# A fp32 decoder trunk on one core: x in five transfers among the first weights, raw rows paired and new queries placed by ScalarE, the norm of x at its old tiles

## The reference

```python
def project_layer(x, pos, norm_g, w_in):
    h = rms_norm(x, norm_g) @ w_in
    pr = dict(zip(IN_NAMES, jnp.split(h, IN_OFFSETS, axis=-1)))
    q_a = rope(pr['q_a'].reshape(b, t, N_DIL * A_HEADS, HEAD_DIM), pos)
    k_a = rope(pr['k_a'].reshape(b, t, N_DIL * A_KV, HEAD_DIM), pos)
    q_c = rope(pr['q_c'].reshape(b, t, C_HEADS, HEAD_DIM), pos)
    kv_c = pr['kv_c'].reshape(b, t, 6, C_KV, HEAD_DIM)
    ...
```

## Time and profile before

| | us |
|---|---|
| median of 3 runs (lowest, highest) | 907.11 (907.03, 907.92) |
| the profiled execution | 908.36 |
| its span | 906.7 |

### The profile page before, as it was taken

One profiled execution on the slowest core, in us unless ns is written; L12 is line 12 of the kernel. 1 busy time (PEld: TensorE's weight loads), 2 busy tenths in 40 slices (PEclk: granted clock), 3 DMA queues, 4 the chain that ended last, 5 costly groups with the idle time before them and its releaser, 6 DMA issues.

```text
span 906.7 us, 21426 instructions
## 1 busy us (share of the span) xinstructions
PE 895.8 (99%) x7902; PEld 839.0 (93%) x7902; DVE 647.0 (71%) x1445; ACT 456.6 (50%) x911; POOL 213.6 (24%) x353
## 2 busy tenths in 40 slices
PE   8999999999999999999999999999999999999997
PEld 8999898888888899999999999889888979999997
DVE  7999776687667567657779996586866575775574
ACT  7444765465543544434544448564654445344352
POOL 3300100347668600000000001013575782000000
PEclk9999999999999999999999999999999999999998
DMA  9761976836989963333566376865659898445321
GB/s 346 278 252 70 416 293 235 328 140 184 348 249 295 339 263 140 140 147 144 232 249 239 142 302 235 346 268 240 206 197 323 257 279 313 169 176 205 131 94 52
DMA packets 65832, 209.97 MB, mean 232 GB/s; under 512 B 12432, under 2 KB 48064, under 8 KB 56384
## 3 DMA queue, kind: packets, MB, share of 16 engines
q1 hardware_dynamic: 55904, 186.49, 56.1%
q0 software_dynamic: 9680, 22.10, 7.6%
q10 hardware_dynamic: 144, 0.01, 0.0%
HBM read 202.58 MB, written 41.36 MB: 269 GB/s over the span
## 4 chain that ended last, share of the span: by engine, by line
PE 91%; ACT 2%; SPq 2%; DVE 2%; issue 2%; DMA 1%; DVEq 0%; ACTq 0%
PE bank L1090 60%; PE bank L1354 11%; PE bank L1103 4%; SPq L879 2%; PE bank L1232 2%; PE bank L1388 1%; PE bank L1261 1%; PE bank L1224 1%; PE bank L1152 1%; DMA big<-in_w_feat 1%; PE bank L1274 1%; PE bank L1485 1%; PE bank L1287 1%; PE bank L1456 1%; PE bank L1415 1%
## 5 line engine op out<-in xcount | busy, mean ns | idle before, releaser
L1877 DVE TENSOR_TENSOR big_r<-big,paged_r 128x1024 fp32r<-128x1024 f32 x156 | 190.7, 1228 | 68.4 <-ACT paged_r L1631 67.4
L1090 PE MATMUL bank<-xnT_high_r,big_r 128*128 128x288 f32 x768 | 226.0, 294 | 0.0
L1090 PE MATMUL bank<-xnT_high_r,paged_r 128*128 128x288 f32 x704 | 212.7, 302 | 0.5 <-DVE oT_a L1983 0.4
L1090 PE MATMUL bank<-xnT_r,paged_r 128*128 128x288 f32 x704 | 207.7, 295 | 0.0
L1631 ACT ACTIVATE paged_r<-big 128x1024 fp32r<-128x1024 f32 x156 | 163.1, 1052 | 4.2 <-DMA big<-in_w_feat 2.8
L1090 PE MATMUL bank<-short_r,big_r 128*128 128x288 f32 x544 | 160.5, 295 | 0.0
L1090 PEld LDWEIGHTS bank<-xnT_high_r,big_r 128*128 128x128 f32 x768 | 144.5, 188 | 0.0
L1090 PEld LDWEIGHTS bank<-xnT_high_r,paged_r 128*128 128x128 f32 x704 | 132.0, 187 | 4.6 <-issue 2.0
L1090 PEld LDWEIGHTS bank<-xnT_r,paged_r 128*128 128x128 f32 x704 | 132.3, 188 | 0.0
L1090 PE MATMUL bank<-short_r,paged_r 128*128 128x288 f32 x416 | 123.9, 298 | 2.0 <-ACT oT_b L1584 1.0
L1090 PE MATMUL bank<-kvp_r,paged_r 128*128 128x288 f32 x416 | 123.3, 296 | 0.0
(11 more groups left out here) (364 smaller groups left out, 1851.3 us busy)
## 6 DMA issues: line engine op xcount, KB each, us to landing
big<-in_w_tok SPq DMA_DIRECT2D x12, 2048.0 KB, 8.7
big<-in_w_feat SPq DMA_DIRECT2D x12, 2048.0 KB, 8.4
big<-in_w_gate SPq DMA_DIRECT2D x10, 2048.0 KB, 8.5
out_kept_dil<-in_cache_dil SPq DMA_DIRECT2D x16, 1020.0 KB, 13.9
paged<-in_pool SPq DMA_DIRECT2D x200, 64.0 KB, 4.6
big<-in_w_up SPq DMA_DIRECT2D x12, 1024.0 KB, 9.4
paged<-in_pool POOLq DMA_DIRECT2D x184, 64.0 KB, 5.1
big<-in_kv_win SPq DMA_DIRECT2D x4, 2048.0 KB, 9.4
```

Source lines behind the costliest of these rows:

```text
L1090: last = mm(out, l, r, start=(c == 0 and i == 0), stop=(c == n - 1 and i == 2))
L1877: v.tensor_tensor(l_part, full, h_part.bitcast(FP32), ALU.subtract)\
```

## The change

It does five things. x is loaded in five transfers: tile 0, tile 1, then pairs; tile 1 now stands behind the first row of weights. TensorE runs 7 warm-up matmuls, not 9. y is made and stored in four parts of two tiles. In layer 0 the norm of x stands at tiles 10, 12, and so on to 24, as in layer 1, and no longer at 14, 16, 18, 20, 22, 23, 24, 25. And three pieces of VectorE's work are taken apart: laying raw rows in pairs moves to ScalarE, two tiles later; the scale of w_gc stays on VectorE but comes at tile 26; and rope adds the new tokens' queries in place with one addition, while ScalarE puts them into qblk two tiles later (`newq`).

```diff
@@ -91,9 +91,10 @@
 ROPE_AT = {4: ("k", 0, 0), 5: ("k", 1, 0), 7: ("k", 0, 1)} | {9 + 4 * t + 2 * h: ("q", t, h) for t in range(4) for h in range(2)}
 ROPE_LATER = {{4: 6, 5: 7, 7: 8}.get(i, i): z for i, z in ROPE_AT.items()}
 SPLIT_AHEAD = 3
-WARM_UP, BEFORE_LAST, BETWEEN = 9, 2, 3
-Y_PARTS = [(0, 2), (2, 4), (4, 6), (6, 7), (7, 8)]
-NORM_AT = [{z: i for i, z in enumerate(places)} for places in ((14, 16, 18, 20, 22, 23, 24, 25), range(10, 26, 2))]
+X_PARTS = ((0, 1), (1, 2), (2, 4), (4, 6), (6, 8))
+WARM_UP, BEFORE_LAST, BETWEEN = 7, 2, 3
+Y_PARTS = [(0, 2), (2, 4), (4, 6), (6, 8)]
+NORM_AT = [{10 + 2 * i: i for i in range(KT)}] * DEPTH
 
 MIX = P + K16 + 3 * NS
 S_MIX, S_WIN = D4, D4 + MIX
@@ -273,8 +274,12 @@
         places = ROPE_AT if layer else ROPE_LATER
         if i in places:
             out.append(("rope",) + places[i])
-        if i == TILES.index(("cmp", 1)):
+        if i == TILES.index(("cmp", 1)) + 2:
             out.append(("pairs",))
+        if i == len(TILES) - 2:
+            out.append(("gcscale",))
+        if i - 2 in places and places[i - 2][0] == "q":
+            out.append(("newq",) + places[i - 2][1:])
     units, feats = prompt_units(), list(FEATS)
     out += [("vturn", 1), ("vturn", 2), ("gc",), ("score", units[0]), ("vturn", 3), ("vturn", 0)]
 
@@ -740,6 +745,7 @@
     ROPED = [s[1:] for s in of("rope")]
     roped = sig("roped", ROPED)
     paired = sig("raw_rows_paired", ["all"])
+    new_placed = sig("new_queries_placed", [z[1:] for z in ROPED if z[0] == "q"])
     gc_scaled = sig("gate_weights_scaled", ["all"])
     tanh_done = sig("tanh_done", [s for s in of("feat") if s[1][0] == "z"])
     u_state = sig("conv_state_ready", ["all"])
@@ -770,7 +776,7 @@
     dchain = nc.alloc_semaphore("dve_link")
     stored, stored_new = nc.alloc_semaphore("prompt_stored"), nc.alloc_semaphore("new_stored")
     copied = nc.alloc_semaphore("caches_copied")
-    x_in = [nc.alloc_semaphore(f"x{i}_in") for i in range(KT // 2)]
+    x_in = [nc.alloc_semaphore(f"x{i}_in") for i in range(len(X_PARTS))]
     first_rounded, first_split = (Signal(nc, "first_rows_" + z, all_of("first")) for z in ("rounded", "split"))
     FIRST_ROWS = ((0, 1), (1, 2), (2, 3), (3, 4), (4, 6), (6, 8))
     first_in = [nc.alloc_semaphore(f"first_rows{i}_in") for i in range(len(FIRST_ROWS))]
@@ -902,7 +908,8 @@
             Now.layer = 0
 
             def load_x(i):
-                sp.dma_start(x[:, 2 * i:2 * i + 2, :], a["x"][:, 2 * i:2 * i + 2, :]).then_inc(x_in[i], 16)
+                tiles = slice(*X_PARTS[i])
+                sp.dma_start(x[:, tiles, :], a["x"][:, tiles, :]).then_inc(x_in[i], 16)
 
             def load_first(i):
                 cols = slice(512 * FIRST_ROWS[i][0], 512 * FIRST_ROWS[i][1])
@@ -914,13 +921,14 @@
 
             load_x(0)
             load_first(0)
+            load_x(1)
             load_first(1)
-            load_x(1)
+            load_x(2)
             load_first(2)
             load_first(3)
-            load_x(2)
+            load_x(3)
             load_first(4)
-            load_x(3)
+            load_x(4)
             load_first(5)
             load_second(0)
             for dst, src in CONSTS:
@@ -1371,6 +1379,7 @@
                                       start=True, stop=True)
                     last.then_inc(*PJ.fill(s))
                 elif k == "sscore":
+                    pe.wait_ge(*new_placed.at((3, 1)))
                     _, hb, what = s
                     wait(pe, SC.is_free(s))
                     if what in ("d4", "mix"):
@@ -1529,7 +1538,7 @@
                     if layer == 0:
                         if i == 0:
                             act.wait_ge(g_in, 16)
-                        act.wait_ge(x_in[i // 2], 16)
+                        act.wait_ge(x_in[[first <= i < end for first, end in X_PARTS].index(True)], 16)
                     else:
                         act.wait_ge(*PJ.is_used(("down", i // 4, i % 4), layer - 1))
                     f(xg_high[:, i, :] if layer < DEPTH else xg[:, i, :], x[:, i, :], ACT.Identity,
@@ -1583,6 +1592,26 @@
                         continue
                     f(dst, proj_bank(s)[:, 0:T], ACT.Copy, scale=SCALE if kind == "q" else 1.0)\
                         .then_inc(*proj_ring(layer, s).release(s))
+                elif k == "pairs":
+                    for kind in range(2):
+                        act.wait_ge(*PJ.is_used(("proj", TILES.index(("cmp", kind)))))
+                    act.wait_ge(*layer_in.at("all"))
+                    for kv in range(KV):
+                        f(cT[:, :, kv, P:P + 16], pe_c[:, :, :], ACT.Copy)
+                        for par in range(2):
+                            pairs = raw_cmp[HD * kv:HD * (kv + 1), :, 0:SEQ].rearrange("p k (n z) -> p k n z", z=2)
+                            last = f(cT[HD * par:HD * (par + 1), :, kv, 0:P], pairs[:, :, :, par], ACT.Copy)
+                    last.then_inc(*paired.inc("all"))
+                elif k == "newq":
+                    t, half = s[1:]
+                    part = slice(2 * half, 2 * half + 2)
+                    act.wait_ge(*roped.at(("q", t, half)))
+                    for kv in range(KV):
+                        rows = slice(HD * kv, HD * (kv + 1))
+                        new = raw_q[t][rows, part, SEQ:T].rearrange("p r (b t) -> p b r t", b=REQ)
+                        out = qblk[rows, t, :, :].rearrange("p h (b k r t) -> p (h b) k r t", b=RB, k=KV, r=REP)
+                        last = f(out[:, :, kv, part, :], new, ACT.Copy)
+                    last.then_inc(*new_placed.inc((t, half)))
                 elif k == "vturn":
                     act.wait_ge(*TR.is_full(s))
                     j = s[1]
@@ -1915,26 +1944,13 @@
                                             by_token(turned[:, :, 0:SEQ]), ALU.add)
                         else:
                             v.tensor_tensor(qTC[:, part, :], plain[:, :, 0:SEQ], turned[:, :, 0:SEQ], ALU.add)
-                        for kv in range(KV):
-                            rows = slice(HD * kv, HD * (kv + 1))
-                            new, new_turned = (z[rows, :, SEQ:T].rearrange("p r (b t) -> p b r t", b=REQ)
-                                               for z in (plain, turned))
-                            out = qblk[rows, t, :, :].rearrange("p h (b k r t) -> p (h b) k r t", b=RB, k=KV, r=REP)
-                            last = v.tensor_tensor(out[:, :, kv, part, :], new, new_turned, ALU.add)
+                        last = v.tensor_tensor(plain[:, :, SEQ:T], plain[:, :, SEQ:T], turned[:, :, SEQ:T], ALU.add)
                     last.then_inc(*roped.inc(s[1:]))
-                elif k == "pairs":
-                    for kind in range(2):
-                        dve.wait_ge(*PJ.is_used(("proj", TILES.index(("cmp", kind)))))
+                elif k == "gcscale":
                     dve.wait_ge(*layer_in.at("all"))
                     v.scalar_tensor_tensor(w_gc[:, :, :], w_gc[:, :, :], 0.5,
                                            gT[:, layer, :].unsqueeze(2).to_broadcast([P, KT, 32]), ALU.mult, ALU.mult)\
                         .then_inc(*gc_scaled.inc("all"))
-                    for kv in range(KV):
-                        last = v.tensor_copy(cT[:, :, kv, P:P + 16], pe_c[:, :, :])
-                        for par in range(2):
-                            pairs = raw_cmp[HD * kv:HD * (kv + 1), :, 0:SEQ].rearrange("p k (n z) -> p k n z", z=2)
-                            last = v.tensor_copy(cT[HD * par:HD * (par + 1), :, kv, 0:P], pairs[:, :, :, par])
-                    last.then_inc(*paired.inc("all"))
                 elif k == "feat":
                     kind, kt = s[1:]
                     if kind == "h":
```

## The result

The changed kernel took 908.96 us (median of 15 runs, 908.42 to 909.95), the kernel before 907.70 in the same sessions (15 runs, 907.03 to 908.17): a ratio of 1.0016, 95% interval 1.0009 to 1.0023. That is within 0.2% of before, and outside the range given (905.9 to 908.3): 1.26 us slower, where I had +0.1.

The account below looks back on a forecast made before the run. TensorE, 91% of the chain, was taken to bound the kernel. Start +0.1, tiles 0, gates' product +0.1 and end -0.1 made +0.1 us: 908.46 profiled, 907.2 against the median, 8 in 10 within 905.9 to 908.3.

Parts of the forecast that it names:

- The start: First 20.4 us: x tiles 2 and 3 issued one issue later but still in time; +0.1 us, bounds -0.2 and +0.5.
- The base: Profiled execution of the kernel before, 908.36 us, with tile 4 waiting until 20.42; the terms were summed against it.
- Gates' product: Layer 0, about 100 us: the late w_gc scale brings a new 0.55 us TensorE wait; net +0.1, bounds -0.47 and +0.3.
- the 0.47 gained ahead of it: First feature weights, layer 0: one norm rounding less on ScalarE lets the value tile's copy end 0.47 us sooner.
- The 0.4 us "issue" piece: An instruction fetch in the chain that can fall elsewhere; with the runs' median, 0.2 us either way.
- Tiles, 0: Tile stage: moved pieces fit ScalarE's gaps and VectorE's savings lie beside matmuls; 0, bounds 0 and +0.2 us.
- layer 1, 0: Same edits in layer 1, where the norm's places stay and the items have about 0.4 us of slack; 0.
- End, -0.1: Last 6 us: merged store ends the issues sooner, but the DMA engines are full; -0.1 us, bounds -0.6 and +0.2.
- the whole -0.5: At the end, by the skill's fixed DMA cost alone: the end would move with the last issue, -0.5 us.
- the 1.66: Time outside the 906.7 us span in the profiled execution: 1.66 us.
- Rival B: First stage, slower: a pause after fewer warm-ups delays TensorE's full pace, to 11.1 us; 907.9, or 909.6 if later; chance 0.11.
- The level: Median of the kernel before, taken as 907.11 us; the forecast against it was 907.2.

Follow-up runs that it names:

- e6: Kernel before with only the changed norm places, pairs and new queries on ScalarE, and the w_gc scale at tile 8, not 26: 907.44 us, ratio 0.9995.
- e9: Kernel before with x tiles 0 and 1 as single transfers, tile 1 issued by ScalarE instead of SyncE: 908.36 us, ratio 1.0007.
- e10: Kernel before with x tiles 0 and 1 as two transfers, both ahead of the first weights row, on SyncE: 908.55 us, ratio 1.0007.
- e1: Kernel before with 7 warm-up matmuls instead of 9, nothing else: 907.96 us, ratio 0.9999.
- e4: Changed kernel with 9 warm-up matmuls instead of 7: 909.39 us, ratio 1.0015 against the kernel before.
- e12: Kernel before with pairs on ScalarE and the w_gc scale on VectorE, both at tile 8, and norm at tiles 10 to 24: 906.80 us, ratio 0.9993.

## Why the prediction was wrong

**The start, +0.1 with bounds -0.2 and +0.5: wrong, +1.0 to +1.1 in the runs (by medians, each with some 0.9 us of interval).** This step failed. I had reasoned that the DMA engines had 0.82 MB queued ahead of x tiles 2 and 3 until 4.9 us, so that an issue at 2.76 was in time. In the changed kernel the engines' share between 4.4 and 7.2 us is 0.82, not 0.95: they ran out, because an issue takes SyncE 0.43 us whether it brings 144 KB or 288. Over the traces x tiles 2 and 3 came 0.9 later (6.9 to 7.8), beyond my bound of +0.5. And the weights rows behind them were not in my sum at all: I priced x tiles 2 and 3 (+0.28 in the pair of traces) and neither the third row (+0.95 there, +1.5 over the traces) nor the fifth (+1.2 and +1.3), behind which VectorE's last run without a pause begins. How much of this the later issues make and how much the two small transfers stays open. The rest of that step held: the first row came 0.4 sooner, as forecast, and gave nothing, because VectorE's run sets the end.

**The base was also off.** Of ten starts of that kind the profiled one was the latest; the usual tile 4 starts at 19.6, not 20.42. Against one trace the changed kernel lost 0.43 there, against the ten 1.2.

**Gates' product, +0.1: right in kind, mis-sized.** The new wait, its place and the 0.47 gained ahead of it were as worked out. The line behind came to +0.63. The two new-query copies took 0.51, not 0.25 (97.34 to 97.87), the round started at 98.37, not 98.1, and the split 0.03 behind its end. My upper bound was +0.3. The product waited 1.03, not 0.55. Moving the scale was no need of the change: with it at tile 8 the same stretch is 6.22 us (e6).

**The 0.4 us "issue" piece: named as noise, it was a gain.** -0.3 to -0.4 in every kernel with a shorter VectorE program. With it the middle is +0.25 in the span. I had called it instruction fetch; no run shows that.

**Tiles, 0; layer 1, 0: right.** The six copies fitted into ScalarE's gap, and no wait came up between tile 5 and tile 26.

**End, -0.1: right in size** (-0.12 in the pair of traces, up to -0.4 in others). The Trainium skill, "DMA: Bandwidth & Descriptors", section "Anatomy of one DMA", gives the fixed 2.0 us that I cited for transfers that GpSimd issues; these are SyncE's. No trace shows the whole -0.5.

**Outside the span: not thought of.** +0.43 of the +1.26. I had carried the 1.66 over. With the start's 1.0 the terms add up to 1.6, 0.3 more than was measured, which is within what the intervals leave open.

**Rival B, the clock: the half pace came, its reason and its price are not shown.** It lasted to 10.1, near the 11.1 worked out. But the pause that I gave as its reason did not bring it in e9 and e10. And neither e1 nor e4 shows a price in the medians. In the changed kernel the data set the end of the stage: ScalarE's copy was done at 20.44 and tile 4 waited for VectorE until 20.85. Where the data are early the clock decides: in e1's trace tile 4 started at 20.45 without a wait, while VectorE's first split was ready at 19.29. The Trainium skill, "TensorE: Matmul & The Clock Gate", Part 1, lets the moment of the rise vary by half a us, as I cited. Here it varied by more: with nine warm-ups, all begun at 1.2, it came between 4.2 (e12) and 7.3 (before, e4).

**The level.** I took 907.11, a median of three runs, and allowed 0.2 for it; over fifteen runs it was 907.70. So 0.59 of the 1.76 us between forecast and result is the level of before, and 1.17 the change. Against 907.70 the range would have ended at 908.9, still just short.
